# Mixing stage of a hybrid diffusion block: attention denominators moved within a pair, GLA tiles before the last centring, last transposes inside the output product, weight splits and loads moved

## The chip, the cores and the metric

The kernel runs on one NeuronCore of a Trainium2 chip. The metric is the device time of one execution in microseconds (us). An execution of its own was also recorded by the hardware profiler; every duration below is from that execution.

## The reference

Two layers, each a feed-forward sublayer, a token-mixing sublayer and a second feed-forward sublayer, over 256 latent tokens and 256 context tokens of width 1024. What matters here is the mixing:

```python
def token_mixing(u, uc, ...):
    pl, pc = split_cols(u @ w_in + b_in), split_cols(uc @ w_in + b_in)
    y_a = windowed_attention(q, k, v, kc, vc, sink)        # 8 heads of 64, softmax with a sink
    y_b = silu(pl[6]) * head_layernorm(o_b, gla_g)          # gated linear attention, 4 heads
    y_c = sigmoid(pl[13]) * head_layernorm(o_c, mlstm_g)    # mLSTM, 4 heads, both directions
    y = concatenate([y_a, y_b, y_c]) @ w_out
```

The softmax divides by the sum of the exponentials and the exponential of the sink. In the first layer the latent and the context tokens are both mixed (T = 512); in the second only the latent tokens are wanted (T = 256). All is float32; the large products are made of three products of float32r halves (a high part and a remainder).

## The kernel before

The kernel is one block with a program for each engine; the programs meet at counting semaphores and nowhere else, so the order within each engine is written out by hand. Weights come in units of at most 128x2048: SyncE loads a unit into one of two `raw` buffers (unit n into n % 2), ScalarE copies it to `w_hi` (`split_hi`, L300), VectorE subtracts to make `w_lo` (`split_lo`, L308) and increments `lo_ready`, which lets SyncE load unit n + 2 and TensorE begin unit n. `split_lo` waits for the `hi_ready` of its own `split_hi`.

A layer's mixing sublayer has three parts. **project**: 21 tiles of `u @ w_in`, with the GLA work between them (`gla_after`), until ScalarE has evicted tile 20 (L765). With tile 20, the last, ScalarE and VectorE also split the first unit of w_out. **mixing**: N = 16 iterations in the first layer, N = 8 in the second, over query blocks of 128 tokens (qb) and pairs of attention heads (j = 0 to 3). Four iterations of one qb are what is called a pair below. **project_out**: eight output tiles, each 24 matmuls into bank 4 or 5, in the order of `OUT_ORDER` (inputs 4, 5, 0 to 3, 6, 7; 4 and 5 are GLA, 0 to 3 attention, 6 and 7 mLSTM).

One iteration i of mixing, by engine:
- TensorE: at i % 4 == 1, from i = 5, `denominators` (L1887, sixteen recorded matmuls that turn the inverse sums of the previous qb) at the start; then `scores(i)` (L1849); `turn(i-1)` (L1861, transposes of the exponentials into banks 2 and 3); `values(i-2)` (L1876); mLSTM `keys_queries` (L1901) and `numerators` (L1919). In the first layer a head takes four iterations, with `keys_queries(h, 0..2)` and `numerators(2h), (2h+1)`; in the second a head takes two, and `numerators` stand ahead of `turn`.
- VectorE: `outputs(qb-1)` at j == 2 (L1170, values times inverse sums, to `y_att`), `heads_done` (L1201 to L1211) when a `numerators` is there, the row maxima of the scores (L1251, L1254), the mLSTM `weights` (L1222, L1226), `turned(i-1)` (L1149), `inverses` (L1162, L1164), `centred` (L1176 to L1184, a layer norm's first half).
- ScalarE: at j == 1 `denominators(qb-1)` first (L859, bank 2 to `den_inv`), the two exponentials (L897), `turned(i-1)` (L847), and `decays` (L873 to L880, the mLSTM decay weights of one head and direction).
- GpSimd makes `xg` from `g_all` (L629), which SyncE spreads from a row in memory (`spread`, L475). Each spread of direction d waits until the decays before it are done (`w_ready`).

`denominators` and `turn` share bank 2. That is why `turn(4)`, `turn(8)`, ... (the first of a qb) wait for `den_ready`, the eviction at L859:

```python
if g == 0:
    wait(pe, m["den_ready"], (i - 4) // Q_TILES + 1 if i % Q_TILES == 0 else 0)
```

The tail, after the last iteration. TensorE: `turn_out(4)`, `turn_out(5)` (L1926, transposes of the GLA outputs), `denominators` of the last qb, the last `values`, then a wait for `y_tok_ready`, `turn_out(6)`, a wait for `yt_full`, `turn_out(7)`, and only then project_out, which waits for `att_ready`. ScalarE: the sigmoid of the gate (L908), the last L859, the square root of the mLSTM variances (L911), and the high parts `u_hi` (L920) in `OUT_ORDER`. VectorE: `heads_done(7)`, `centred(3)`, `gated_out(4)`, `gated_out(5)` (L1305), `outputs` of the last qb, reciprocal and normalization (L1320, L1323, `y_tok`), `low` (L1312, the remainders `u_lo`) of 4, 5, 0, 1, 2, 3, `gated_out(6)`, `gated_out(7)`, `low(6)`, `low(7)`.

SyncE: w_out unit 0, then two spreads, unit 1, unit 2, then the six other spreads, unit 3.

Of the kernel before, what the change touches and what calls it, by code (L numbers as in the profile page):

```python
# [13 lines left out]
P = 128  # L14
# [103 lines left out]
def hybrid_block_kernel(nc, x, c, ctx_in, c_ctx, ada_w, ada_b, norm_g, ffn1_wg, ffn1_wu, ffn1_wd, ffn2_wg, ffn2_wu,  # L118
# [3 lines left out]
    with ExitStack() as stack:  # L122
# [257 lines left out]
        TURN_BANKS = {4: 5, 5: 6, 6: 7, 7: 5}  # L380
# [16 lines left out]
        def _(sp):  # L397
# [46 lines left out]
            for layer in range(DEPTH):  # L444
# [34 lines left out]
                for u in range(KT // 2):  # L479
# [5 lines left out]
                    if u == KT // 2 - 1:  # L485
                        for hd in range(2, 2 * C_HEADS):
                            spread(hd)
# [169 lines left out]
        def _(act):  # L657
# [92 lines left out]
            def project(layer, m, T):  # L750

                n0 = first_unit["in", layer]
                for t in range(N_PROJ):
                    u = t // 2
                    if t % 2 == 0 and t > 0:
                        split_hi(act, n0 + u + 1)
# [78 lines left out]
            def mixing(layer, m, T):  # L835
# [50 lines left out]
                for i in range(N):  # L886
                    qb, j = i // Q_TILES, i % Q_TILES
                    W = TOK if qb < 2 else CTX
                    if j == 1 and qb > 0:
                        denominators(qb - 1)  # L890
# [8 lines left out]
                    if i >= 1:  # L899
                        turned(i - 1)  # L900
                    h, step = (i + lead) // per_head, (i + lead) % per_head
# [8 lines left out]
                act.wait_ge(m["ml_ln"], 5 * C_HEADS)  # L910
                nc.scalar.activation(ml_s[:, 2, :, 0:NQ], ml_s[:, 1, :, 0:NQ], ACT.Sqrt, bias=eps_col[:], scale=1.0 / 64)\  # L911
                    .then_inc(m["ml_sqrt"], 1)
                for f in OUT_ORDER:
                    if f < Q_TILES:
                        act.wait_ge(m["att_ready"], NQ)
                        src = y_att[:, f, 0:T]
                    else:
                        act.wait_ge(m["yt_full"], f - 3)
                        src = tmp_b[f % 2][:, 0:T]
                    nc.scalar.activation(u_hi[:, f, 0:T], src, ACT.Copy).then_inc(m["yt_hi"], 1)  # L920
# [59 lines left out]
        def _(dve):  # L980
# [152 lines left out]
            def mixing(layer, m, T):  # L1133
# [103 lines left out]
                for i in range(N):  # L1237
# [24 lines left out]
                    if per_head == 4:  # L1262
# [13 lines left out]
                        if step == 2 and h > 0:  # L1276
                            centred(h - 1)
                    if per_head == 2 and step == 1 and h < C_HEADS:
# [19 lines left out]
                centred(C_HEADS - 1)  # L1298
# [19 lines left out]
                outputs(NQ - 1)  # L1318
                dve.wait_ge(m["ml_sqrt"], 1)
# [7 lines left out]
                for f in (4, 5, 0, 1, 2, 3):  # L1327
                    low(f)
# [24 lines left out]
            def project(layer, m, T):  # L1353

                n0 = first_unit["in", layer]
                for t in range(N_PROJ):
                    if t % 2 == 0 and t > 0:
                        split_lo(dve, n0 + t // 2 + 1)
# [192 lines left out]
        def _(pe):  # L1551
# [261 lines left out]

            def project_out(layer, m, z, T):
                n0 = first_unit["out", layer]
                pe.wait_ge(m["att_ready"], T // P)
                for u in range(KT // 2):
                    s = begin(n0 + u)
                    for t in range(2 * u, 2 * u + 2):
                        wait(pe, post["y_ready"], KT * z + t - 1)  # L1820
                        for e, k in enumerate(OUT_ORDER):
                            if t == 0:
# [7 lines left out]
            def mixing(layer, m, T):  # L1830
# [21 lines left out]
                def turn(i):  # L1852

                    n = 4 if i // Q_TILES < 2 else 2
                    for g in range(A_GROUPS):
                        pe.wait_ge(m["exp_done"], 2 * i + g + 1)
                        wait(pe, m["pt_dve"] if g else m["pt_act"], i)
                        if g == 0:
                            wait(pe, m["den_ready"], (i - 4) // Q_TILES + 1 if i % Q_TILES == 0 else 0)
# [20 lines left out]
                def denominators(qb):  # L1880

                    pe.wait_ge(m["den_step"], 2 * qb + 2)
                    pe.wait_ge(m["pt_act"], Q_TILES * (qb + 1))
# [39 lines left out]
                def turn_out(f):  # L1923

                    for tt in range(NQ):
                        last = nc.tensor.transpose(bank[TURN_BANKS[f]][:, tt * P:(tt + 1) * P],  # L1926
                                                   y_tok[:, tt, (f - Q_TILES) * P:(f - Q_TILES + 1) * P], ident[:])
                    last.then_inc(m["yt_turned"], 1)

# [12 lines left out]
                for i in range(N + 2):  # L1942
                    h, step = (i + lead) // per_head, (i + lead) % per_head
                    if i % Q_TILES == 1 and i >= Q_TILES:
                        denominators(i // Q_TILES - 1)
                    if i < N:
                        scores(i)
                    if i == 0:
                        turn_values()
# [13 lines left out]
                    if i == N:  # L1963
                        pe.wait_ge(m["p_ready"], pair_done(T, C_HEADS - 1, n_groups - 1, 1))
                        turn_out(4)
                        turn_out(5)
                    if per_head == 4 and step > 0 and h < C_HEADS:
# [6 lines left out]
                pe.wait_ge(m["y_tok_ready"], 2 * (T // LAT))  # L1974
                turn_out(6)
                pe.wait_ge(m["yt_full"], 1)
                turn_out(7)
# [104 lines left out]
```

## Time and profile before

| | us |
|---|---|
| median of 3 runs (2002.73 to 2006.70) | 2004.55 |
| profiled execution, its own time | 2008.94 |
| profiled execution, span from first to last instruction | 2007.1 |
| TensorE busy | 1873.5 (93%) |
| VectorE busy | 1109.3 (55%) |
| ScalarE busy | 760.1 (38%) |
| GpSimd busy | 243.6 (12%) |

The mixing iterations of the first layer run from 604.5 to 707.7 us of the span, those of the second from 1698.1 to 1751.9 us; the eight tiles of project_out follow each. Feed-forward work fills nearly all of the rest. The time of a row is where an instruction begins. A duration is that of the whole merged group (x4 is four instructions), and the value in brackets is how long the engine had been idle, with what released it. The granted clock is 1.00 at 2.4 GHz and 0.50 at 1.2 GHz.

### The profile page before, as it was taken

Reading aid. Unit: us, or ns where it says so; the run is one execution under the profiler, and the core shown is the slowest. Engines: PE = TensorE matmul, PEld = TensorE weight load, DVE = VectorE, ACT = ScalarE, POOL = GpSimd, SP = SyncE. Lnnn points to the kernel's source line nnn. Section 1 sums busy time; section 2 is a strip of 40 time slices with the busy share of each in tenths; the row PEclk is TensorE's granted clock in tenths of the full one; section 3 lists DMA queues with packets and bytes.
Section 4 is the critical chain, followed back from the end, with each engine's and each line's share of the span. In section 5 each row is a group of like instructions: output and inputs, shape, how many; then the busy total and the mean of one; then the engine's idle time right before and its main releaser. Section 6 shows DMA issues by size and latency. Waiting matters only on the chain. (4 is left out here: it accounts for less than half of the span.)

```text
span 2007.1 us, 25666 instructions
## 1 busy us (share of the span) xinstructions
PE 1873.5 (93%) x10461; PEld 1521.9 (76%) x10461; DVE 1109.3 (55%) x1630; ACT 760.1 (38%) x1132; POOL 243.6 (12%) x327
## 2 busy tenths in 40 slices
PE   5999999979998886999999979999999799879998
PEld 3788877857786664888778858887888488769997
DVE  1777722245756646777522267775222676855544
ACT  4423222236436445222313253222232645654443
POOL 4011110012531000111110001110000152000000
PEclk7999999989999797999999979999999799979999
DMA  9566654342321022666553416665234243036654
GB/s 298 147 180 196 178 160 141 96 113 43 85 64 43 11 63 63 202 178 191 168 173 87 115 49 202 178 194 153 79 94 113 65 106 84 13 105 165 178 166 122
DMA packets 366469, 254.05 MB, mean 127 GB/s; under 512 B 30610, under 2 KB 343276, under 8 KB 366352
## 3 DMA queue, kind: packets, MB, share of 16 engines
q1 hardware_dynamic: 345648, 182.97, 33.1%
q0 software_dynamic: 20704, 69.44, 10.8%
q8 instruction: 83, 1.36, 0.3%
q14 instruction: 34, 0.28, 0.0%
HBM read 251.30 MB, written 1.07 MB: 126 GB/s over the span
## 5 line engine op out<-in xcount | busy, mean ns | idle before, releaser
L324 PE MATMUL bank<-u_hi,w_hi 128*128 128x512 f32 (+2 forms) x1872 | 690.8, 369 | 29.7 <-DVE u_lo L1000 20.6
L325 PE MATMUL bank<-u_lo,w_hi 128*128 128x512 f32 (+2 forms) x1872 | 682.8, 365 | 0.0
L326 PE MATMUL bank<-u_hi,w_lo 128*128 128x512 f32 (+2 forms) x1872 | 682.5, 365 | 0.0
L308 DVE TENSOR_TENSOR w_lo<-raw,w_hi 128x2048 fp32r<-128x2048 f32 (+2 forms) x182 | 373.0, 2049 | 262.3 <-ACT w_hi L300 262.1
L324 PEld LDWEIGHTS bank<-u_hi,w_hi 128*128 128x128 f32 (+1 forms) x1872 | 357.8, 191 | 110.8 <-issue 51.6
L326 PEld LDWEIGHTS bank<-u_hi,w_lo 128*128 128x128 f32 (+1 forms) x1872 | 357.5, 191 | 56.8 <-issue 0.9
L325 PEld LDWEIGHTS bank<-u_lo,w_hi 128*128 128x128 f32 (+1 forms) x1872 | 358.1, 191 | 53.8 <-issue 0.5
L300 ACT ACTIVATE w_hi<-raw 128x2048 fp32r<-128x2048 f32 (+2 forms) x182 | 311.8, 1713 | 144.0 <-PE bank L326 126.6
L324 PE MATMUL bank<-ht_hi,w_hi 128*128 128x512 f32 (+1 forms) x704 | 256.8, 365 | 1.4 <-DVE w_lo L308 1.4
L326 PE MATMUL bank<-ht_hi,w_lo 128*128 128x512 f32 (+1 forms) x704 | 255.3, 363 | 0.0
L325 PE MATMUL bank<-ht_lo,w_hi 128*128 128x512 f32 (+1 forms) x704 | 255.2, 363 | 0.0
L715 ACT ACTIVATE tmp_a<-bank 128x512 f32<-128x512 f32 (+1 forms) x88 | 47.9, 544 | 537.1 <-PE bank L326 537.1
L1034 DVE SCALAR_TENSOR_TENSOR ada_sum<-ada_slot,silu_c,ada_sum 128x512 f32<-128x512 f32 x336 | 230.7, 746 | 0.0
L512 POOL DMA_DIRECT2D ada_slot<-in_ada_w_dram x128 | 92.1, 720 | 936.3 <-DVE ada_sum L1034 655.1
L1053 DVE TENSOR_TENSOR tmp_b<-bank,tmp_a 128x512 f32<-128x512 f32 (+1 forms) x88 | 55.0, 625 | 210.9 <-ACT tmp_a L715 210.9
L324 PEld LDWEIGHTS bank<-ht_hi,w_hi 128*128 128x128 f32 x704 | 132.8, 189 | 27.6 <-issue 6.7
L326 PEld LDWEIGHTS bank<-ht_hi,w_lo 128*128 128x128 f32 x704 | 132.8, 189 | 20.7
L325 PEld LDWEIGHTS bank<-ht_lo,w_hi 128*128 128x128 f32 x704 | 132.9, 189 | 20.4
L724 ACT ACTIVATE tmp_a<-bank 128x512 f32<-128x512 f32 (+1 forms) x48 | 25.3, 527 | 206.6 <-PE bank L326 206.6
L1075 DVE TENSOR_TENSOR tmp_b<-tmp_b,tmp_a 128x512 f32<-128x512 f32 (+1 forms) x36 | 21.7, 604 | 124.0 <-ACT tmp_a L724 124.0
L1056 DVE TENSOR_TENSOR ht_lo<-tmp_b,ht_hi 128x512 fp32r<-128x512 f32 (+1 forms) x88 | 55.1, 626 | 56.7 <-ACT ht_hi L717 56.7
L717 ACT ACTIVATE ht_hi<-tmp_b 128x512 fp32r<-128x512 f32 (+1 forms) x88 | 50.9, 578 | 61.1 <-DVE tmp_b L1053 61.1
(244 smaller groups left out, 1486.4 us busy)
## 6 DMA issues: line engine op xcount, KB each, us to landing
ada_slot<-in_ada_w_dram POOLq DMA_DIRECT2D x128, 512.0 KB, 4.7
raw<-in_ffn_wg_dram SPq DMA_DIRECT2D x88, 512.0 KB, 4.8
raw<-in_ffn_wu_dram SPq DMA_DIRECT2D x88, 512.0 KB, 6.2
raw<-in_ffn_wd_dram SPq DMA_DIRECT2D x64, 384.0 KB, 3.4
raw<-in_ffn_wd_dram SPq DMA_DIRECT2D x64, 320.0 KB, 4.0
raw<-in_w_in_dram SPq DMA_DIRECT2D x32, 512.0 KB, 4.3
ada_first<-in_ada_w_dram SPq DMA_DIRECT2D x4, 2048.0 KB, 14.8
raw<-in_w_in_dram SPq DMA_DIRECT2D x16, 256.0 KB, 4.3
```

Of the source, the lines that this page charges most:

```text
L300: nc.scalar.activation(w_hi[s][:, 0:size], raw[s][:, 0:size], ACT.Copy).then_inc(hi_ready[s], 1)
L308: nc.vector.tensor_tensor(w_lo[s][:, 0:size], raw[s][:, 0:size], w_hi[s][:, 0:size].bitcast(F32), ALU.subtract).then_inc(lo_ready[s], 1)
L324: nc.tensor.matmul(acc, wh, xh, start=first, stop=False)
L325: nc.tensor.matmul(acc, wh, xl, start=False, stop=False)
L326: return nc.tensor.matmul(acc, wl, xh, start=False, stop=last)
L512: pool.dma_start(ada_slot[slot][:], src[:, 2 * r:2 * r + 2, b * BLOCK:(b + 1) * BLOCK]).then_inc(ada_loaded[slot], 16)
L715: nc.scalar.activation(tmp_a[j][:, 0:T], bank[2 * j][:, 0:T], ACT.Silu).then_inc(gated["silu_ready"], 1)
L717: nc.scalar.activation(ht_hi[:, f, 0:T], tmp_b[j][:, 0:T], ACT.Copy).then_inc(gated["hthi_ready"], 1)
L724: nc.scalar.activation(tmp_a[b][:, 0:T], bank[4 + b][:, 0:T], ACT.Square).then_inc(post["ysq_ready"], 1)
L1034: ins = nc.vector.scalar_tensor_tensor(acc[:], ada_slot[slot][:, kk, :], c_k, acc[:], ALU.mult, ALU.add)
L1053: nc.vector.tensor_tensor(tmp_b[j][:, 0:T], bank[2 * j + 1][:, 0:T], tmp_a[j][:, 0:T], ALU.mult).then_inc(gated["prod_ready"], 1)
L1056: nc.vector.tensor_tensor(ht_lo[:, f, 0:T], tmp_b[j][:, 0:T], ht_hi[:, f, 0:T].bitcast(F32), ALU.subtract).then_inc(gated["ht_ready"], 1)
```

## The change

1. **Denominators at the end of a pair's first iteration.** TensorE issues them at the end of iteration 5, 9, 13 (and N + 1) and no longer at the start; ScalarE evicts them after `turned(i-1)` and ahead of `decays` (before, ahead of the exponentials by position, but behind the `decays` of the iteration before). The wait for `den_ready` moves from the `turn` of iterations 4, 8, 12 to that of 5, 9, 13, and `outputs` stay at j == 2.
2. **`keys_queries(0, 2)`** moves from the end of iteration 1 to behind `scores(2)`, in the first layer only.
3. **First w_out unit.** Its `split_hi` and `split_lo` leave tile 20 of project for iteration 2 of mixing, in both layers. On ScalarE it stands behind `turned(1)`; on VectorE behind `turned(1)` in the first layer and ahead of `weights` and `turned(1)` in the second.
4. **SyncE** issues the six other spreads ahead of w_out unit 2 (before: behind it).
5. **Tail.** VectorE: `gated_out(4)`, `(5)`, `outputs`, `low` of 4, 5, 0, 1, then `centred(3)`, `low` of 2, 3, then reciprocal and `y_tok`. ScalarE's square root moves behind the `u_hi` of 4, 5, 0 to 3. TensorE's `turn_out(6)` and `(7)` move into the first output tile, between inputs 3 and 6; bank 0 instead of 5 takes the second, and its wait for `yt_full` goes.
6. A second wait for `proj_ready` ahead of `turn_values`; the one ahead of the loop stays.

```diff
-        TURN_BANKS = {4: 5, 5: 6, 6: 7, 7: 5}
+        TURN_BANKS = {4: 5, 5: 6, 6: 7, 7: 0}
...
-                    if u == KT // 2 - 1:
+                    if u == 2:
                         for hd in range(2, 2 * C_HEADS):
                             spread(hd)
...
-                    if t % 2 == 0 and t > 0:
+                    if t % 2 == 0 and 0 < t < N_PROJ - 1:
                         split_hi(act, n0 + u + 1)
...
-                    if j == 1 and qb > 0:
-                        denominators(qb - 1)
                     if j == 0 and qb > 0:
                         sink_terms(qb - 1)
...
                     if i >= 1:
                         turned(i - 1)
+                    if i == 2:
+                        split_hi(act, first_unit["out", layer])
+                    if j == 1 and qb > 0:
+                        denominators(qb - 1)
...
-                act.wait_ge(m["ml_ln"], 5 * C_HEADS)
-                nc.scalar.activation(ml_s[:, 2, :, 0:NQ], ...)
                 for f in OUT_ORDER:
+                    if f == 6:
+                        act.wait_ge(m["ml_ln"], 5 * C_HEADS)
+                        nc.scalar.activation(ml_s[:, 2, :, 0:NQ], ...)
...
                         if step == 2 and h > 0:
                             centred(h - 1)
+                    if i == 2:
+                        split_lo(dve, first_unit["out", layer])
                     if per_head == 2 and step == 1 and h < C_HEADS:
                         weights(h, 0, 0)
...
                 heads_done(2 * C_HEADS - 1)
-                centred(C_HEADS - 1)
...
                 outputs(NQ - 1)
+                for f in (4, 5, 0, 1):
+                    low(f)
+                centred(C_HEADS - 1)
+                for f in (2, 3):
+                    low(f)
                 dve.wait_ge(m["ml_sqrt"], 1)
...
-                for f in (4, 5, 0, 1, 2, 3):
-                    low(f)
...
-                    if t % 2 == 0 and t > 0:
+                    if t % 2 == 0 and 0 < t < N_PROJ - 1:
                         split_lo(dve, n0 + t // 2 + 1)
...
                         for e, k in enumerate(OUT_ORDER):
+                            if t == 0 and k == 6:
+                                pe.wait_ge(m["y_tok_ready"], 2 * (T // LAT))
+                                turn_out(6, T)
+                                turn_out(7, T)
                             if t == 0:
                                 pe.wait_ge(m["yt_ready"], e + 1)
...
-                        if g == 0:
-                            wait(pe, m["den_ready"], (i - 4) // Q_TILES + 1 if i % Q_TILES == 0 else 0)
+                        if g == 0 and i % Q_TILES == 1:
+                            wait(pe, m["den_ready"], i // Q_TILES)
...
-                    pe.wait_ge(m["pt_act"], Q_TILES * (qb + 1))
+                    pe.wait_ge(m["pt_act"], min(Q_TILES * (qb + 1) + 1, N))
...
-                    if i % Q_TILES == 1 and i >= Q_TILES:
-                        denominators(i // Q_TILES - 1)
                     if i < N:
                         scores(i)
+                    if per_head == 4 and i == 2:
+                        keys_queries(0, 2)
                     if i == 0:
+                        pe.wait_ge(m["proj_ready"], N_PROJ)
                         turn_values()
...
-                    if per_head == 4 and step > 0 and h < C_HEADS:
+                    if per_head == 4 and step > 0 and h < C_HEADS and i != 1:
                         keys_queries(h, step - 1)
...
-                pe.wait_ge(m["y_tok_ready"], 2 * (T // LAT))
-                turn_out(6)
-                pe.wait_ge(m["yt_full"], 1)
-                turn_out(7)
+                    if i % Q_TILES == 1 and i >= Q_TILES:
+                        denominators(i // Q_TILES - 1)
```

## Rows read from the trace of the kernel before

**Rows 1.** The page, part 1: busy time (share of the span) xinstructions.

```profile
PE 1873.5 (93%) x10461; PEld 1521.9 (76%) x10461; DVE 1109.3 (55%) x1630; ACT 760.1 (38%) x1132; POOL 243.6 (12%) x327
```

**Rows 2.** Stretches: length, busy PE, PEld, DVE, ACT, POOL, clock, DMA share, GB/s.

```profile
604.50:707.70 103.20, 89.83 (x648) 67.77 (x649) 68.53 (x209) 55.72 (x163) 7.61 (x6) 0.87 0.10 27
612.90:619.80 6.90, 6.90 (x32) 4.72 (x32) 4.17 (x12) 2.65 (x8) 2.53 (x2) 0.53 0.18 40
681.20:701.70 20.50, 20.50 (x98) 16.56 (x98) 8.73 (x31) 5.41 (x14) 0.00 (x0) 0.51 0.01 1
707.70:720.50 12.80, 12.78 (x51) 10.06 (x49) 7.70 (x10) 3.51 (x4) 0.00 (x0) 0.87 0.20 49
1698.10:1751.90 53.80, 48.39 (x417) 38.10 (x417) 44.14 (x150) 35.94 (x94) 4.38 (x6) 1.00 0.14 35
1751.90:1759.40 7.50, 7.47 (x51) 7.27 (x48) 5.42 (x10) 2.78 (x4) 0.00 (x0) 0.77 0.00 1
```

**Rows 3.** Timeline, TensorE, first stage, opening: start, duration, operation, [idle before <-releaser].

```profile
612.79 1.64 PE L1901 MATMUL bank<-qk_conv 64*128 64x256 f32 x3 [2.25 <-DVE w_c L1226]
```

**Rows 4.** Timeline, ScalarE then VectorE, first stage, opening.

```profile
602.05 1.91 ACT L300 ACTIVATE w_hi<-raw 128x2048 fp32r<-128x2048 f32 x1
...
603.99 2.29 DVE L308 TENSOR_TENSOR w_lo<-raw,w_hi 128x2048 fp32r<-128x2048 f32 x1 [3.35 <-ACT w_hi L300]
```

**Rows 5.** Waits of the first stage: total us, times, longest.

```profile
DVE probs_t L1149 <- PE bank L1861: 7.5, 4, 5.9
...
PE bank L1861 <- ACT den_inv L859: 3.5, 3, 1.3
```

**Rows 6.** Timeline, TensorE, ScalarE, VectorE, first stage, around denominators.

```profile
631.93 1.13 PE L1901 MATMUL bank<-qk_conv 64*128 64x256 f32 x4
...
634.15 1.09 PE L1887 MATMUL bank<-ident,row_sum 128*64 128x128 f32 x16 [1.08 <-ACT probs_t L847]
...
639.55 0.48 PE L1901 MATMUL bank<-qk_conv 64*128 64x256 f32 x1 [0.29 <-DVE w_c L1226]
...
636.45 0.58 ACT L859 ACTIVATE den_inv<-bank 128x512 f32<-128x512 f32 x1
...
636.43 0.69 DVE L1251 CUSTOM_DVE_ANT_0 probs<-bank,att_mask 128x512 f32<-128x512 f32 x1 [0.71 <-PE bank L1849]
...
640.61 0.68 DVE L1170 TENSOR_TENSOR y_att<-bank,den_inv 128x512 f32<-128x512 f32 x1
...
678.08 0.76 DVE L1254 TENSOR_REDUCE row_max<-bank 128x1 f32<-128x256 f32 x2 [0.25 <-PE bank L1849]
```

**Rows 7.** Timeline, TensorE then VectorE, first stage, tail.

```profile
706.87 1.09 PE L1926 MATMUL bank<-ident,y_tok 128*128 128x128 f32 x8 [3.68 <-DVE y_tok L1323]
...
707.72 0.48 PE L324 MATMUL bank<-u_hi,w_hi 128*128 128x512 f32 x1
...
714.88 0.39 PE L324 MATMUL bank<-u_hi,w_hi 128*128 128x512 f32 x1
...
711.78 1.35 DVE L1312 TENSOR_TENSOR u_lo<-tmp_b,u_hi 128x512 fp32r<-128x512 f32 x2
```

**Rows 8.** Timeline, ScalarE then VectorE, second stage, opening.

```profile
1711.15 0.57 ACT L847 ACTIVATE probs_t<-bank 128x512 f32<-128x512 f32 x1
...
1709.60 0.62 DVE L1226 SCALAR_TENSOR_TENSOR w_c<-bank,w_c 128x256 f32<-128x256 f32 x2
...
1714.71 0.69 DVE L1251 CUSTOM_DVE_ANT_0 probs<-bank,att_mask 128x512 f32<-128x512 f32 x1
...
1719.94 0.69 DVE L1251 CUSTOM_DVE_ANT_0 probs<-bank,att_mask 128x512 f32<-128x512 f32 x1 [1.00 <-DVE hid_tmp L1211]
```

**Rows 9.** Timeline, TensorE then VectorE, second stage, tail.

```profile
1751.47 0.66 PE L1926 MATMUL bank<-ident,y_tok 128*128 128x128 f32 x4 [2.62 <-DVE y_tok L1323]
...
1756.34 0.28 PE L324 MATMUL bank<-u_hi,w_hi 128*128 128x256 f32 x1
...
1754.31 0.82 DVE L1312 TENSOR_TENSOR u_lo<-tmp_b,u_hi 128x256 fp32r<-128x256 f32 x2
```

More of the change, by code:

```diff
@@ L909, in mixing @@
                 denominators(NQ - 1)
-                act.wait_ge(m["ml_ln"], 5 * C_HEADS)
-                nc.scalar.activation(ml_s[:, 2, :, 0:NQ], ml_s[:, 1, :, 0:NQ], ACT.Sqrt, bias=eps_col[:], scale=1.0 / 64)\
-                    .then_inc(m["ml_sqrt"], 1)
                 for f in OUT_ORDER:
+                    if f == 6:
+                        act.wait_ge(m["ml_ln"], 5 * C_HEADS)
+                        nc.scalar.activation(ml_s[:, 2, :, 0:NQ], ml_s[:, 1, :, 0:NQ], ACT.Sqrt, bias=eps_col[:], scale=1.0 / 64)\
+                            .then_inc(m["ml_sqrt"], 1)
                     if f < Q_TILES:
@@ L1812, in gla_after, with turn_out @@
                         last.then_inc(m["gate_turned"], 1)
+            def turn_out(f, T):
+                m = mixer
+                for tt in range(T // P):
+                    last = nc.tensor.transpose(bank[TURN_BANKS[f]][:, tt * P:(tt + 1) * P],
+                                               y_tok[:, tt, (f - Q_TILES) * P:(f - Q_TILES + 1) * P], ident[:])
+                last.then_inc(m["yt_turned"], 1)
             def project_out(layer, m, z, T):
@@ L1921, in numerators @@
                     last.then_inc(m["num_done"], 1)
[L1923 to L1928, printed above, removed]
                 def turn_values():
@@ L1964, in mixing @@
                         pe.wait_ge(m["p_ready"], pair_done(T, C_HEADS - 1, n_groups - 1, 1))
-                        turn_out(4)
-                        turn_out(5)
-                    if per_head == 4 and step > 0 and h < C_HEADS:
+                        turn_out(4, T)
+                        turn_out(5, T)
+                    if per_head == 4 and step > 0 and h < C_HEADS and i != 1:
                         keys_queries(h, step - 1)
```

## The prediction

> **What bounds the kernel.** I read the page first: TensorE is busy 93% of the span [rows 1], so only what TensorE waits for can be had. Then the stretches of both mixing stages: the first is 103.2 us with TensorE busy 89.8 of them at a granted clock of 0.87, the second 53.8 us with 48.4 busy at 1.00 [rows 2]. The change touches only these stages and the first output tile behind each. The idle time, 13.4 and 5.4 us, is the direct stake, and the clock a second one: the first stage holds two stretches at 1.2 GHz, 6.9 us and 20.5 us long, in which TensorE is shown as busy throughout [rows 2]. Then the waits and the timelines, engine by engine. At the ends of the pairs and in both tails TensorE waits for VectorE or ScalarE, which wait for TensorE in turn, so a step has to be followed through the three queues.
>
> **Opening of the first stage.** keys_queries(0, 2) makes TensorE wait 2.25 us for VectorE's weights with scores(2) ready behind it, and then the clock is at 0.53 for 6.9 us [rows 2, 3]. With scores(2) ahead, the gap shrinks to some 0.4 us in pieces: 1.9 us gained. If the clock then stays up, the 6.9 us at 0.53 become 3.8: 3.1 more. Against that stands the split of the first w_out unit, now in iteration 2: 1.91 us on ScalarE and then 2.29 us on VectorE, which has to wait for it [rows 4]. Queued behind it on VectorE is heads_done(0). TensorE meanwhile has scores(3), turn(2), values(1) and keys_queries(1, 0), four groups of about 1.1 us [rows 6], and comes to numerators(1), which need heads_done(0), at the same moment; on ScalarE the exponentials of iteration 4 come to stand behind decays(2) and lose 1.0. Leaving tile 20 gains 0.1: the eviction of tile 20 waits for its matmuls anyway, and TensorE's start hangs on that; what goes from VectorE there (2.29 us) has TensorE's own turn_values and keys_queries as its cover. Sum: -1.9 - 3.1 + 1.0 = **-4.0 us** (bounds: -5.0, and 0 if the clock falls all the same and the stall costs more).
>
> **Denominators, first stage, three times.** Removed: TensorE's wait for the 0.58 us eviction, which stands behind decays on ScalarE (3.5 us in three), and the 1.08 us and its like ahead of L1887 [rows 5, 6]. But TensorE only reaches keys_queries(h, 2) sooner, and that waits for VectorE's weights(h, 0, 1) as it does now (idle 0.29 [rows 6]). VectorE gains where it waited for the late scores and turns: 0.71, 0.25, and three waits of 1.6 together (7.5 less the longest, 5.9, which belongs to the tail): 2.6 in all [rows 5, 6]. It loses at outputs: these now follow keys_queries (1.05), denominators (1.05) and the eviction (0.58 and 0.1 of handing over), 2.8 us behind weights(h, 0, 1), where it has 1.1 us of its own (639.55 to 640.61 [rows 6]). That is 1.7 us of new waiting each time, and the row maxima, the weights of the third group and numerators are queued behind it. 3 x 1.65 - 2.55 = **+2.4 us** (bounds: +5, and -3.5 if only the removed wait counted).
>
> **Tail of the first stage.** VectorE's queue sets it: today it runs without a gap to the last remainder, 711.78 + 1.35 = 713.1, and the second output tile starts at 714.88 [rows 7]. Its instructions are the same; two waits are new. centred(3), some 2.1 us, was the cover for denominators and their eviction; now outputs stand there, and values(15) comes ahead of denominators: 1.4 us of waiting. Then y_tok to turn_out(6) to gated_out(6), now without the remainders as a cover: 0.6. The output product does start earlier (about 705.2 for 707.72 [rows 7]), but its inputs 6 and 7 come last and later: last remainder 715.1, second tile at 715.9: **+1.0 us** (bounds: -2.5, the earlier start kept whole; +2.5).
>
> **Opening of the second stage.** Here split_lo stands ahead of weights(1, 0, 0), which starts at 1709.60. ScalarE comes to split_hi at 1711.15 + 0.5 [rows 8]; 1.91 and 2.29 us [rows 4] end at 1715.8. So VectorE is 6.2 us late. A wait for the transposes absorbs some 0.5, the idle 1.00 ahead of 1719.94 [rows 8] nearly all of another microsecond; the rest passes from max(3) (1714.71 [rows 8]) to everything behind it, since each engine waits for the one before: **+4.8 us** (bounds: 0, cover after all; +6.2). What it leaves in project (the split in tile 20) ran beside that tile's matmuls: 0. TensorE, ready for numerators(2) at 1713.3, stands until 1717.0, 3.7 us. The gaps of 2.25, 3.68 and 2.62 us [rows 3, 7, 9] were each followed by some time at 1.2 GHz: the stretches at 0.53, 0.87 and 0.77 [rows 2]. So I price a clock fall here at what it costs if it is as short as the first: TensorE's three groups before it needs VectorE again take 3.6 us more, of which 1.7 lies in a wait: **+1.9 us** (bounds: 0, and +9 if it is like the stretch of 20.5 us).
>
> The Trainium skill's page "TensorE: Matmul & The Clock Gate" (Why this matters for your kernels) asks for no long idle gap between bursts of matmuls, and its part on a second failure mode says that short idles between groups can make the clock swing too. The trace agrees with the second: 2.25 us was enough.
>
> **Second stage, the rest.** Denominators once: outputs are 1.1 us later, but the scores behind them come late too; **0** (bounds +-1.1). Tail: the same two waits, 1.3 and 0.5 us; the last remainder goes from 1754.31 + 0.82 to 1756.9, the second tile from 1756.34 [rows 9] to 1757.3: **+1.0 us** (bounds: -1.5, +2).
>
> **SyncE, GpSimd and the doubled wait: 0.** The six spreads no longer stand behind w_out unit 2 and its load; xg comes earlier. Unit 2 now loads behind the last spread, half a stage later, and has the second half of mixing and the products of two w_out units as cover; if that were not enough, TensorE would wait ahead of the fifth output tile. The second wait for proj_ready is behind one that it repeats.
>
> **Sum.** -4.0 + 2.4 + 1.0 + 4.8 + 1.9 + 0 + 1.0 = **+7.1 us**. The profiled execution took 2008.94 us (span 2007.1), 0.2% above the median; I add the sum to the median: 2004.55 + 7.1 = **2011.6 us**, +0.35%. A measurement of this kernel can tell about 0.2% (4.0 us) from no change.
>
> **Rivals.**
> - *The clock stays up* (faster). The place is the first stage from 681 us on: 20.5 us at 0.51, TensorE busy all the time [rows 2]. At 1.00 this is 10.2 us less, and with no fall in the second stage 1.9 less again: 2011.6 - 12.1 = 1999.5. For it: the gaps ahead of L1887 and of turn at the third pair end go. Against: in their place comes one of some 2.4 us ahead of keys_queries(h, 2), and the 2.25 us gap was followed by a fall. It decides if no gap of more than 2 us is followed by one. 0.15.
> - *The clock falls more often.* There are three gaps of 2.2 to 2.6 us now in the first stage and 3.7 in the second, each a candidate by the same rows; one further stretch like that of 20.5 us costs 10: 2021. By the skill's advice on idle gaps this is the danger of the change. 0.15.
> - *The split in the second stage is covered* (the wait costs nothing): 2011.6 - 4.8 - 1.9 = 2004.9. For: VectorE is busy 44 of 53.8 us, not all [rows 2]. Against: ScalarE cannot start it before 1711.6, and VectorE's queue waits in order. 0.12.
> - *The tails gain what they are meant to*, the product's earlier start: -2.5 and -1.2 for +1.0 and +1.0: 2005.9. Against: VectorE's queue has no gap to lose today. 0.08.
> - *It does not do what it says*: only the doubled wait, which does nothing; no time in it.
>
> **Chances and range.** The forecast has 0.50; its own range is 2006 to 2016, and 0.08 of the 0.50 lies within 0.2% of 2004.55. Slower by over 0.2%: 0.42 of it and the 0.15 of the second rival, 0.57. Faster: 0.11 of the first rival's 0.15 (its 1999.5 is 0.25% below) and 0.03 of the third's, 0.14. Within 0.2%: 0.08, 0.04, 0.09 of the third and the 0.08 of the fourth, 0.29. The range, 2001 to 2020, takes in both covers and most of one long fall, and leaves out the better half of the first rival and the worse half of the second.
>
> **What would show it.** In the first stage: no gap of 2 us ahead of L1901 at its start, numerators(0) 5 us sooner; VectorE waiting for den_inv ahead of L1170 by 1.5 us three times. In the second: VectorE idle for 4 us ahead of L308, and TensorE idle for 3 to 4 us ahead of L1919. In the tails: TensorE starts L324 sooner by 2.5 and 1 us, then waits for u_lo, and the second tile starts 1 us later against turned of the last iteration. I am wrong if VectorE does not wait in the second stage, or if the stretches at 1.2 GHz change their sum by more than 7 us.

## The result and the profile after

The changed kernel took 2018.71 us (median of 4 runs, 2016.79 to 2024.21), the kernel before 2004.03 us beside it (2002.73 to 2006.70). The ratio is 1.0076, 95% interval 1.0054 to 1.0098: slower by 14.7 us, inside the range of the prediction, 7.1 us above its forecast. The recorded execution took 2024.21 us.

The page of the changed kernel, span and part 1:

```profile
span 2022.4 us, 25670 instructions
PE 1879.8 (93%) x10461; PEld 1522.8 (75%) x10461; DVE 1110.3 (55%) x1630; ACT 761.3 (38%) x1132; POOL 243.6 (12%) x327
```

The number of instructions is that of [rows 1] on every engine, and DVE and ACT are busy 1.0 and 1.2 us more. PE is busy 6.3 us more with the same 10461 matmuls, so more of them ran at the lower clock; the rest of the 15.3 us that the span grew is waiting. Stretches of the changed kernel: first stage up to the first output product, two short pieces of it, that product; then the second stage likewise. The short pieces are windows set around stretches at 1.2 GHz and begin 0.4 us after them (length, busy PE, PEld, DVE, ACT, POOL, clock, DMA share, GB/s):

```profile
607.50:702.10 94.60, 81.77 (x640) 59.70 (x640) 66.03 (x199) 55.09 (x159) 7.61 (x6) 0.95 0.11 29
640.50:643.90 3.40, 3.40 (x16) 1.56 (x13) 1.56 (x4) 0.60 (x1) 0.65 (x1) 0.56 0.00 0
684.90:688.30 3.40, 3.40 (x23) 2.32 (x23) 0.55 (x2) 0.60 (x1) 0.00 (x0) 0.56 0.00 0
702.10:721.90 19.80, 14.41 (x56) 10.84 (x57) 11.86 (x21) 7.83 (x13) 0.00 (x0) 0.91 0.20 54
1699.20:1761.50 62.30, 52.61 (x412) 41.60 (x412) 44.20 (x143) 35.65 (x92) 4.36 (x6) 0.92 0.11 31
1719.10:1725.90 6.80, 6.22 (x38) 5.88 (x38) 6.17 (x21) 2.58 (x8) 0.72 (x1) 0.53 0.02 4
1761.50:1775.00 13.50, 10.39 (x52) 9.61 (x52) 8.05 (x19) 5.96 (x12) 0.00 (x0) 0.62 0.10 25
```

The kernel before, each stage from its first scores to the start of the third output tile, where TensorE waits for the eviction of the first (Y_mix):

```profile
604.50:721.90 117.40, 102.61 (x696) 77.83 (x696) 76.65 (x219) 60.61 (x170) 7.61 (x6) 0.87 0.12 32
1698.10:1760.30 62.20, 55.86 (x464) 45.39 (x465) 49.86 (x160) 39.61 (x100) 4.38 (x6) 0.97 0.12 31
```

**The first stage became shorter, the second much longer.** Up to the third output tile the first takes 114.3 us for 117.4, clock 0.95 in its loop for 0.87; the second takes 75.8 us (1699.28 to 1775.06) for 62.2. That is -3.1 and +13.6 of the 15.3 us. The rest lies outside of the change: +3.0 ahead of the first stage, +1.3 between the stages and +0.5 behind. There the two recorded executions differ in their stretches at 1.2 GHz: 15 us more of them in all in the changed kernel (mean granted clock 0.949 for 0.953), none of it in the two stages.

The second stage's loss starts in its third iteration. Timeline of the changed kernel, ScalarE, then VectorE, then TensorE:

```profile
1712.80 1.90 ACT L300 ACTIVATE w_hi<-raw 128x2048 fp32r<-128x2048 f32 x1
...
1714.73 2.29 DVE L308 TENSOR_TENSOR w_lo<-raw,w_hi 128x2048 fp32r<-128x2048 f32 x1 [3.87 <-ACT w_hi L300]
1716.94 0.62 DVE L1229 SCALAR_TENSOR_TENSOR w_c<-bank,w_c 128x256 f32<-128x256 f32 x2
...
1719.24 0.29 DVE L1210 TENSOR_TENSOR hid_tmp<-bank,c_den 128x128 f32<-128x128 f32 x1
...
1721.78 0.69 DVE L1254 CUSTOM_DVE_ANT_0 probs<-bank,att_mask 128x512 f32<-128x512 f32 x1
...
1719.68 3.22 PE L1938 MATMUL bank<-vm_tok,w_c 128*128 128x65 f32 x14 [5.08 <-DVE hid_tmp L1210]
1722.70 1.91 PE L1880 MATMUL bank<-ident,probs 128*128 128x128 f32 x8
```

VectorE idles 3.87 us for ScalarE's half of the split, then works 2.29 us on its own, and everything of the iteration stands behind both: the row maxima of iteration 3 (L1254) start 22.5 us into the stage, before 16.6. TensorE idles 5.08 us, and what it waits for at the end is `hid_tmp` of heads_done(1) at 1719.24, six entries behind the weights at 1716.94 in VectorE's queue. The clock falls while it still waits, at 1718.7, and stays at 1.2 GHz for 6.8 us.

At the ends of the pairs in the first stage, TensorE and VectorE of the changed kernel ([rows 6] show the same place before: L1901 is now L1920, L1887 is L1906, L1170 is L1173):

```profile
638.47 1.13 PE L1920 MATMUL bank<-qk_conv 64*128 64x256 f32 x4 [2.04 <-DVE w_c L1229]
639.53 1.46 PE L1906 MATMUL bank<-ident,row_sum 128*64 128x128 f32 x16
640.92 2.08 PE L1868 MATMUL bank<-proj 64*128 64x512 f32 x4
...
641.65 0.69 DVE L1173 TENSOR_TENSOR y_att<-bank,den_inv 128x512 f32<-128x512 f32 x1 [2.05 <-ACT den_inv L859]
...
662.83 1.13 PE L1920 MATMUL bank<-qk_conv 64*128 64x256 f32 x4 [2.68 <-DVE w_c L1229]
...
683.77 1.41 PE L1920 MATMUL bank<-qk_conv 64*128 64x256 f32 x4 [1.97 <-DVE w_c L1229]
```

The waits ahead of L1887 and of turn are gone, and TensorE waits 2.0 to 2.7 us ahead of keys_queries(h, 2) instead of 0.29. Each of the three is followed by a stretch of 3.4 us at 1.2 GHz (from 640.1, 664.0 and 684.5; two stand in the stretches above). The long one of 20.5 us [rows 2] is not there. Waits (total us, times, longest) of the same kernel in that stage:

```profile
DVE y_att L1173 <- ACT den_inv L859: 7.6, 4, 2.8
```

### The profile page after: what moved, and what is told of

Same layout as the page of the kernel before. It is cut to its first block and busy times, and to the rows that moved or that the text cites. A ratio compares the mean times of both kernels' runs of the same rounds, so it can differ in the third digit from the quotient of the medians.

```text
span 2022.4 us, 25670 instructions
## 1 busy us (share of the span) xinstructions
PE 1879.8 (93%) x10461; PEld 1522.8 (75%) x10461; DVE 1110.3 (55%) x1630; ACT 761.3 (38%) x1132; POOL 243.6 (12%) x327
## 5 line engine op out<-in xcount | busy, mean ns | idle before, releaser
L308 DVE TENSOR_TENSOR w_lo<-raw,w_hi 128x2048 fp32r<-128x2048 f32 (+2 forms) x182 | 373.0, 2050 | 262.4 <-ACT w_hi L300 262.1
L325 PEld LDWEIGHTS bank<-ht_lo,w_hi 128*128 128x128 f32 x704 | 132.9, 189 | 20.5
L326 PEld LDWEIGHTS bank<-ht_hi,w_lo 128*128 128x128 f32 x704 | 132.8, 189 | 20.5
```

The lines of the kernel that those rows point to most:

```text
L308: nc.vector.tensor_tensor(w_lo[s][:, 0:size], raw[s][:, 0:size], w_hi[s][:, 0:size].bitcast(F32), ALU.subtract).then_inc(lo_ready[s], 1)
L325: nc.tensor.matmul(acc, wh, xl, start=False, stop=False)
L326: return nc.tensor.matmul(acc, wl, xh, start=False, stop=last)
```

## The experiments

All are compared with runs of the kernel before on the same chip. Times and ratios are from all runs; stage times are from the one recorded execution of each kernel, in two parts: the loop, from the stage's first scores to VectorE's last copy of transposed exponentials, and the tail, from there to the third output tile. Kernels measured on different chips are compared by their ratios.

**The split alone, and everything but the split.** e1 is the changed kernel with the split back in tile 20:

```diff
-                    if t % 2 == 0 and 0 < t < N_PROJ - 1:
+                    if t % 2 == 0 and t > 0:
...
-                    if i == 2:
-                        split_hi(act, first_unit["out", layer])
...
-                    if i == 2:
-                        split_lo(dve, first_unit["out", layer])
```

> The changed kernel with the first w_out unit split in tile 20 of project again, in both layers; all else as changed. Theory S (VectorE's wait for ScalarE's split ahead of weights in the second mixing stage is the largest part of the loss: max(4) came 7.9 us later against the first scores): the time falls by 7 to 10 us from the changed kernel's 2018.7, to 2009 to 2012, and TensorE's gap of 5.1 us ahead of numerators(2) is gone. Rival C (the loss is in the clock and in the tails, wherever the split stands): falls by less than 3 us, to 2016 or more.

e2 is the opposite: these edits, and the order of the spreads, on the kernel before.

> The kernel before with the split in iteration 2 of mixing in both layers, and the spreads ahead of w_out unit 2; nothing else. Theory S: slower than before by 6 to 10 us (2010 to 2014), nearly all of it in the second stage, where VectorE waits some 4 us for the split. In the first stage TensorE still waits ahead of keys_queries(0, 2), so the stall costs up to 1 to 2 us there. Rival C: within 3 us of 2004.

Measured: e1 2009.87 us, ratio 1.0025 (1.0010 to 1.0040), for 1.0076 of the changed kernel: without the split 8.8 us of the 14.7 are gone by the medians, some 10 us by the ratios. e2 2016.86 us, 1.0060 (1.0040 to 1.0080): alone it costs 12 us. In e1 the second stage takes 68.2 us, 7.6 less than in the changed kernel. In e2 the second stage takes 56.5 + 14.9 us for 47.3 + 14.9 of before: +9.2, all of it in the loop. Its timeline, VectorE then TensorE, repeats what the changed kernel showed (L1209 is heads_done here):

```profile
1708.97 2.29 DVE L308 TENSOR_TENSOR w_lo<-raw,w_hi 128x2048 fp32r<-128x2048 f32 x1 [3.87 <-ACT w_hi L300]
...
1713.92 3.22 PE L1923 MATMUL bank<-vm_tok,w_c 128*128 128x65 f32 x14 [5.09 <-DVE hid_tmp L1209]
```

**The tail alone, and everything but the tail.** e3 is the changed kernel with part 5 of the change taken back, e4 the kernel before with part 5 alone. The core of e4:

```diff
-                centred(C_HEADS - 1)
...
+                for f in (4, 5, 0, 1):
+                    low(f)
+                centred(C_HEADS - 1)
+                for f in (2, 3):
+                    low(f)
...
+                            if t == 0 and k == 6:
+                                pe.wait_ge(m["y_tok_ready"], 2 * (T // LAT))
+                                turn_out(6, T)
+                                turn_out(7, T)
```

> The changed kernel with the tail of before (centring, y_tok and the last transposes ahead of the output product). Theory T (the new tail costs 1 us in each stage by VectorE's two new waits, and some of the clock on top: from the last turned the second output tile came 1.5 and 2.3 us later): faster than the changed kernel by 2 to 5 us, 2014 to 2017. Rival (the tail gains its earlier start of the output product, and the losses behind it are the clock's own): slower than the changed kernel by 0 to 3 us.

> The kernel before with the new tail alone. Theory T: slower than before by 1.5 to 4 us (2005.5 to 2008): VectorE waits for den_inv ahead of L1170 about 0.8 to 1.4 us and for turn_out(6) 0.8 to 1 us, in both stages. Here denominators still stand ahead of the last values, so the first of these waits is shorter by up to 1 us than in the changed kernel. Rival: faster by 2 to 4 us, as the output product starts 2.5 and 1.2 us earlier.

Measured: e3 2016.84 us, 1.0066 (1.0047 to 1.0084), some 2 us better than the changed kernel, within what the runs can tell. The expectation had 2 to 5 us. e4 2014.24 us, 1.0038 (1.0015 to 1.0062), its twelve times in two groups: five of 1999.0 to 2006.8 us at granted clocks of 0.960 to 0.962, and seven of 2011.4 to 2022.0 us at 0.950 to 0.956. The recorded execution is of the first (2003.9 us). In it the second tail takes 17.0 us for 14.9, +2.1; the first takes 23.0 us, what it took before. Two more records of the same kernel, e9 and e10 below, have 18.0 and 24.6 us, +3.1 and +1.7. In both, a stretch at 1.2 GHz falls on the second output tile of the first tail; in e4 it lies earlier, where TensorE waits. TensorE's gaps in that second tail:

```profile
1742.11 0.35 PE L324 MATMUL bank<-u_hi,w_hi 128*128 128x256 f32 x1 [1.29 <-DVE u_lo L1312]
...
1744.85 0.38 PE L324 MATMUL bank<-u_hi,w_hi 128*128 128x256 f32 x1 [1.09 <-DVE u_lo L1312]
...
1748.08 0.58 PE L324 MATMUL bank<-u_hi,w_hi 128*128 128x256 f32 x1 [1.32 <-DVE u_lo L1312]
```

One wait of 2.62 us for y_tok [rows 9] became three for remainders, 3.7 us together: TensorE starts the product earlier and still waits for VectorE's remainders.

**The denominators alone.** e5 is the kernel before with part 1 of the change:

```diff
-                    if i % Q_TILES == 1 and i >= Q_TILES:
-                        denominators(i // Q_TILES - 1)
                     if i < N:
                         scores(i)
...
+                    if i % Q_TILES == 1 and i >= Q_TILES:
+                        denominators(i // Q_TILES - 1)
```

> The kernel before with the denominators moved, alone. Theory D (in its new place the chain keys_queries, denominators, eviction, outputs leaves TensorE a gap of 2 to 2.7 us ahead of keys_queries(h, 2) and VectorE a wait of 1.7 us ahead of outputs): slower than before by 3 to 7 us, of which 2 to 3 us are the waits and the rest the clock after the gaps; in the second stage, up to the last turned, 0 to 1 us. Rival (the removed wait for the eviction, 3.5 us in three, is gained): faster by 2 to 4 us.

Measured: 2011.01 us, 1.0030 (1.0018 to 1.0041). Timeline of e5, TensorE in the first stage:

```profile
616.28 1.46 PE L1901 MATMUL bank<-qk_conv 64*128 64x256 f32 x3 [2.25 <-DVE w_c L1226]
642.00 1.13 PE L1901 MATMUL bank<-qk_conv 64*128 64x256 f32 x4 [2.18 <-DVE w_c L1226]
666.48 1.13 PE L1901 MATMUL bank<-qk_conv 64*128 64x256 f32 x4 [2.79 <-DVE w_c L1226]
```

The first row is the old gap of the opening [rows 3]; the others are new. And VectorE waits 7.1 us in three ahead of L1170:

```profile
DVE y_att L1170 <- ACT den_inv L859: 7.1, 3, 2.7
```

The second stage takes 48.7 + 16.3 us: +1.3 in the loop and +1.4 in the tail. The cost by the ratio is 6.0 us, by the medians 7.6.

**keys_queries(0, 2) alone.**

```diff
+                    if per_head == 4 and i == 2:
+                        keys_queries(0, 2)
...
-                    if per_head == 4 and step > 0 and h < C_HEADS:
+                    if per_head == 4 and step > 0 and h < C_HEADS and i != 1:
```

> The kernel before with keys_queries(0, 2) behind scores(2), alone. Theory K: TensorE's gap of 2.25 us ahead of L1901 falls to some 0.5 us, faster than before by 1 to 4 us (1.9 us of waiting, and 0 to 3 of the clock). Rival: no change, since VectorE and not TensorE sets the pace there.

Measured: 2000.66 us, 0.9986 (0.9973 to 0.9998): the one part that gains, some 2.8 us. TensorE's 2.25 us gap is now in two pieces:

```profile
613.08 1.13 PE L1901 MATMUL bank<-qk_conv 64*128 64x256 f32 x4 [0.75 <-DVE w_c L1226]
617.32 2.44 PE L1919 MATMUL bank<-vm_tok,w_c 128*128 128x65 f32 x20 [0.90 <-DVE w_c L1226]
```

The first stage's loop takes 83.8 us in it. In e2 and e4, which have the old opening, it takes 85.1, so the move is worth 1.3 us of that loop.

**Is it the clock or VectorE's queue?** e7 is the changed kernel with seven products that nobody uses in TensorE's 5.1 us gap of the second stage, so that TensorE does not stand still there:

```diff
+                        if i == 3:
+                            pe.wait_ge(m["pt_act"], 2)
+                            for r in range(7):
+                                nc.tensor.matmul(bank[T_BANK][:, 0:TOK], ident[:], proj[:, T_K, :], start=True, stop=True)
```

> The changed kernel, in whose second stage TensorE runs seven idle products of 128x512 (identity by keys into bank 2, some 3.7 us) in the gap of 5.1 us ahead of numerators(2), so that only the clock can change. If the clock's fall is part of what the split costs (9.2 us up to the last turned, where the wait alone is worth some 5.5 to 6): faster than the changed kernel by 2 to 4 us, and TensorE's first numerators after the gap take 1.8 us instead of 3.2. If the fall comes all the same or costs nothing, as VectorE sets the pace: within 1 us.

e8 is the changed kernel with VectorE's half of the split at the end of iteration 2 in place of ahead of the weights:

```diff
-                    if i == 2:
-                        split_lo(dve, first_unit["out", layer])
                     if per_head == 2 and step == 1 and h < C_HEADS:
                         weights(h, 0, 0)
...
+                    if i == 2:
+                        split_lo(dve, first_unit["out", layer])
```

> The changed kernel with VectorE's half of the split at the end of iteration 2 (behind weights, turned, heads_done and centred of the second stage); ScalarE's half stays. Theory S (it is the wait of VectorE for ScalarE, with weights and turned queued behind it, not the 2.29 us of the subtraction): faster than the changed kernel by 5 to 8 us; the wait of 3.9 us ahead of L308 is gone and TensorE's gap ahead of numerators(2) too. Rival (any place in the second stage costs the same, as VectorE is the bound there): faster by less than 3 us.

TensorE of e7 in the gap, and VectorE then TensorE of e8:

```profile
1709.47 6.28 PE L1974 MATMUL bank<-proj,ident 128*128 128x512 f32 x14
1715.58 1.67 PE L1938 MATMUL bank<-vm_tok,w_c 128*128 128x65 f32 x14
1717.09 1.04 PE L1880 MATMUL bank<-ident,probs 128*128 128x128 f32 x8
```

```profile
1714.42 2.29 DVE L308 TENSOR_TENSOR w_lo<-raw,w_hi 128x2048 fp32r<-128x2048 f32 x1
...
1719.24 1.77 PE L1920 MATMUL bank<-qk_conv 64*128 64x256 f32 x7 [2.50 <-DVE w_c L1229]
```

In e7 the clock stays up: the numerators behind the gap take 1.67 us and not 3.22. The first row maxima of iteration 4 are done 29.2 us into the stage, where the changed kernel has 31.0 and the kernel before 23.2. But the stage ends only 1.2 us sooner, though it holds 10 us less at 1.2 GHz. The time is 2018.30 us, 1.0060 (1.0045 to 1.0076): by the ratios up to 3 us better than the changed kernel, which the runs can't tell from nothing. The test is not a clean one: the products took 6.28 us and not the expected 3.7, so the numerators start 1.0 us later against the stage's start than in the changed kernel. Without that the clock could be worth up to 1.0 us more (an estimate from these two starts). In e8 VectorE has no wait at the split, TensorE's gap is 2.50 us, the loop takes 52.3 us for 56.9, and the time is 2015.90 us, 1.0055 (1.0037 to 1.0073), between its two expectations. **VectorE's queue carries the loss; the clock adds 1 to 2 us here, 3 at most.** Even in a better place the split costs: the row maxima of iteration 3 come 2.2 us later in e8 than before, which is the 2.29 us of the instruction itself. The rest of what e8's second stage loses, 8.9 us in all, is not taken apart; it holds the moved denominators and the new tail too.

**The two groups of e4.** The same kernel, recorded twice more.

> The kernel before with the tail edits alone, once more, for its profile. Its twelve timed runs lay in two groups, 1999 to 2006 us and 2014 to 2022 us, and the one recorded execution was of the first group (2003.9 us, granted clock 0.960; second stage 47.5 us to its last transposed exponentials, 2.1 us more than before from there to the second of project_out's units). Theory C (the clock alone makes the second group): a recorded execution of the second group has the same stages within 1 us wherever the granted clock is the same, and the 12 us more are stretches at 1.2 GHz, some 24 us of them more in all. Theory T (the tail edit itself has two outcomes): the 12 us lie behind the last iteration of one of the two stages, at an unchanged clock. If this execution is of the first group, nothing is decided.

> The same kernel and the same two theories as the run before it: by theory C an execution near 2017 us differs from one near 2004 us by some 24 us more at 1.2 GHz, wherever they lie; by theory T the 12 us lie behind the last iteration of one of the stages at the same clock. Two executions of the first group would leave it open.

2006.52 and 2011.60 us. Neither is near 2017, so the groups stay unexplained. What they show is what the clock does with equal work. TensorE in the second stage of e4's record, and then the same place in e9:

```profile
1734.68 1.75 PE L1934 MATMUL bank<-vm_tok,w_c 128*128 128x65 f32 x14 [1.94 <-DVE hid_tmp L1212]
```

```profile
1735.36 2.91 PE L1934 MATMUL bank<-vm_tok,w_c 128*128 128x65 f32 x13 [1.93 <-DVE hid_tmp L1212]
```

The stretch of e9 that begins there:

```profile
1735.80:1742.60 6.80, 6.80 (x41) 6.09 (x40) 1.90 (x8) 2.51 (x3) 0.00 (x0) 0.52 0.01 2
```

One and the same gap was followed by no fall in e4 and by 6.8 us at 1.2 GHz in e9 and e10; their loop takes 49.5 us for 47.5. And e9 and e10 are equal within 0.1 us in every part of both stages; the 5.1 us between them lie ahead of the first stage, where e10 spends 10.2 us more at 1.2 GHz. That is as the theory of the clock has it, for 5 us and not for 12. It is not so everywhere: e9 has 3.4 us at 1.2 GHz (from 694.4) at the start of the first tail that e10 has not, and both tails take 24.6 us, since TensorE has waits there.

**A better place for the eviction, and the split in one layer.** e11 has keys_queries(0, 2) as e6 and, on ScalarE alone, `denominators(qb - 1)` right behind `turned(i - 1)` at j == 0 in the first layer:

```diff
-                    if j == 1 and qb > 0:
+                    if j == 1 and qb > 0 and per_head == 2:
                         denominators(qb - 1)
...
+                    if j == 0 and qb > 0 and per_head == 4:
+                        denominators(qb - 1)
```

> The kernel before with two edits: keys_queries(0, 2) behind scores(2), as in the run that had this alone (2000.7 us, ratio 0.9986), and in the first stage ScalarE evicts the denominators right behind the turned of the last iteration of a pair, ahead of its decays, while TensorE issues them where it did before. Theory D (the 1.1 us gaps ahead of the first turn of a query block, three of them, are a real loss): 2 to 3 us less than with the first edit alone, 1998 us. Theory V (VectorE and ScalarE set the pace there, and the eviction in its new place makes ScalarE wait for TensorE with its decays behind it): the same as the first edit alone or up to 3 us more, 2000 to 2004 us, with new gaps ahead of keys_queries.

e12 has the split in iteration 2 in the first layer only, and the spreads' order in both:

```diff
-                    if t % 2 == 0 and t > 0:
+                    if t % 2 == 0 and 0 < t < N_PROJ - (T == TOK):
...
+                    if i == 2 and T == TOK:
+                        split_lo(dve, first_unit["out", layer])
```

> The kernel before with the split of the first w_out unit moved to iteration 2 of mixing in the first layer alone; in the second layer it stays with tile 20. The six spreads go ahead of w_out unit 2 in both. With the move in both layers it was 2016.9 us (ratio 1.0060). Theory S (the whole cost of the move lies in the second stage): the second stage is back at 47.3 us to its last transposed exponentials, and the time is that of the kernel before, 2002 to 2007 us. Rival (the order of the spreads and loads, or the first stage, costs too): 2008 us or more, with the second stage or project_out waiting for a load.

e11: 2012.06 us, 1.0027 (1.0008 to 1.0046), worse than both theories had it. TensorE's gaps of its first stage:

```profile
638.08 0.48 PE L1903 MATMUL bank<-qk_conv 64*128 64x256 f32 x1 [0.86 <-DVE w_c L1228]
...
660.48 0.91 PE L1903 MATMUL bank<-qk_conv 64*128 64x256 f32 x3 [1.52 <-DVE w_c L1228]
664.67 2.45 PE L1921 MATMUL bank<-vm_tok,w_c 128*128 128x65 f32 x20 [1.47 <-DVE w_c L1228]
...
681.39 0.79 PE L1903 MATMUL bank<-qk_conv 64*128 64x256 f32 x1 [1.96 <-DVE w_c L1228]
```

The 1.3 us ahead of turn are gone and stand ahead of keys_queries(h, 2) again: in this kernel as in e5 and the changed one, the wait taken from TensorE there comes back ahead of VectorE's weights. This record also has the 20.5 us stretch, from 681.2, at the end of the last of these gaps, and its loop takes 94.7 us. e12: 2003.08 us, 0.9990 (0.9974 to 1.0006), no difference, and the loop of its second stage takes 47.7 us, near the 47.3 of before. In the first layer the split and the order of spreads and loads cost nothing that the runs can tell, though VectorE waits there too (2.20 us at its `split_lo`):

```profile
623.63 2.29 DVE L308 TENSOR_TENSOR w_lo<-raw,w_hi 128x2048 fp32r<-128x2048 f32 x1 [2.20 <-ACT w_hi L300]
```

The fastest kernel is e6, faster than the one before by 0.14% (at least 0.02%) and faster than the changed one by 18 us.

## Why the prediction was right, and where it was not

The sign and the range were right, with 14.7 us for the forecast's 7.1. By its own steps:

**Opening of the second stage, +4.8 and +1.9.** The mechanism was the right one and the largest term: ScalarE's half late, VectorE waiting 3.87 us ahead of L308 ("idle for 4 us") and then working. The size was off: 9.2 us in e2 for 6.7. Two steps failed. "A wait for the transposes absorbs some 0.5, the idle 1.00 nearly all of another microsecond": nearly nothing is absorbed of the 6.2 us. In e2 the row maxima of iteration 3 come 5.9 us later than before, and in e7, with the clock held up, those of iteration 4 still 6.0 us later. And "TensorE, ready for numerators(2), stands until 1717.0, 3.7 us" named the weights as the last thing awaited, where it is heads_done(1), six instructions further down VectorE's queue: 5.08 us. The clock term, +1.9, has the right size: 6.8 us at 1.2 GHz followed, and e7 puts its worth at 1.2 (end of the stage) to 1.9 us (row maxima of iteration 4), or up to 1.0 more for the products' late end.

**Second stage, the rest, 0 and +1.0.** Together they were too low. "Outputs are 1.1 us later, but the scores behind them come late too" holds for the loop within its bound (+1.3 in e5). But denominators at the end of iteration N + 1 also delay the tail by 1.4 us, which had no term of its own. The tail term was counted to the second output tile; there e4 is 1.2 us later than before, near the forecast's 1.0, and the changed kernel 2.3. To the third tile e4 loses 2.1 us. Split, denominators and tail measured alone make 9.2 + 2.7 + 2.2 = 14.1 us in this stage; together they made 13.6. So in these records the parts add up. That rests on which record of the tail edits is taken: in e9 and e10 they cost the stage 5.3 us and not 2.2, with 6.8 us more at 1.2 GHz.

**Denominators in the first stage, +2.4.** The step was right: TensorE would "only reach keys_queries(h, 2) sooner", and VectorE would wait for den_inv. The waits are larger: 2.4 us each in e5 (7.1 in three) where I had 1.7, and 2.0 to 2.7 us ahead of keys_queries. The cost by the ratio is 6.0 us for e5, less 2.7 for the second stage: some 3.3. By the recorded loops it depends on what it is held against: 92.4 us in e5 against 94.5 before, or against 85.1 in e4 and e9, which have the loop of before unchanged.

**That is the trap of the base.** The recorded execution of before had the stretch of 20.5 us at 0.51 [rows 2], and the same loop without it takes 85.1 us, 9.3 less. I noted that this execution was 0.2% above the median and used the stretch as a rival's stake, but it comes and goes between executions: e4, e9 and e10, with the same loop, don't have it, nor have e2 and e6; e11 and e12 do. The kernel before itself was recorded only once. So the first stage of the changed kernel looks 3.1 us better than before in the two profiles, while its loop takes 4.3 us more than that of e4, and by the runs only the move of keys_queries gains anything there.

**Opening of the first stage, -4.0.** Right in sign. (6.9 us at 0.53 are 3.7 us at full clock, so the -3.1 should have been -3.2; nothing hangs on it.) The split's +1.0 is 0 (85.12 us in e2 with it, 85.10 in e4 without; e12 0.9990). Of the gain, -1.9 and -3.1, the runs show -2.8 together with bounds of -0.4 and -5.4 (e6). **Tail of the first stage, +1.0**: to the second tile 0.0 in e4 and +1.5 us in the changed kernel; to the third 0.0 in e4 and +1.7 in e9 and e10. The term is about as large as what the clock does to it. **SyncE and the doubled wait, 0**: right for the spreads (e12); the wait was not tried by itself.

**What does not add up.** By the ratios the four parts measured alone make 12.0 (split) + 6.0 (denominators) + 7.6 (tail) - 2.8 (keys_queries) = 22.8 us, together 15.2. Most of the difference is in the tail edits: 7.6 us when they stand alone, 2.0 when they are taken out of the changed kernel (e3). No run shows why, and e4's two groups belong to the same open question. So it is in part luck that the measured time lies in the forecast's range: the second stage was forecast at +7.7 us and took +13.6, and the first, forecast at -0.6, shows -3.1 against the record of before and +6.2 against that of e4.

**The rivals.** "The clock stays up" did not come: in the recorded execution the long stretch was not there, and short ones were. Up to the third output tiles the two stages have seven, 34 us together, where the kernel before had four, also 34 us: so the net loss between the two profiles in these stages is not a longer time at 1.2 GHz. By this the prediction's own sign of being wrong (a change of more than 7 us) is not met in the stages; outside of them it is, with 15 us more, and 4.8 us of the span. "It falls more often" named the mechanism that did come, with gaps of 2.0 to 2.7 and 5.1 us all followed by a fall, and its 2021 is nearer to the result than the forecast; but its further long stretch did not come, and e7, which held the clock up at the longest gap, did not change the time beyond what the runs can tell. The Trainium skill's page "TensorE: Matmul & The Clock Gate" (Why this matters for your kernels) advises against long idle gaps; here the clock stayed at 1.00 when the 5.1 us gap was filled with products that do nothing, and no time clear of the noise came back. "The split is covered" was excluded for the second layer by e2 beside e12, and held in the first; "the tails gain" was excluded by e4, whose ratio is above 1 by its whole interval.

## What to carry to other kernels

A pair of instructions on two engines, the second waiting for the first, costs the second engine's in-order queue the whole wait plus its own time: put it where that queue idles, and look in each layer separately, since the same move was free in one and cost 9 us in the other, its clock fall included. To price such a stall, follow the queue to the last thing that the third engine needs, not the first. And before a trace is used as a base, compare its stretches at the lower clock with a second record of the same code: here a loop took 94.5 us in one record and 85.1 in three others.

## What the runs showed of the hardware

The same instructions of one kernel with the same gap (1.93 and 1.94 us) were followed by a fall of the granted clock in two executions and by none in a third. Over the 68 runs of the kernel before beside the experiments, the time (1999 to 2014 us) follows the mean granted clock, some 1.4 us for 0.001 of it (a straight line through them). In one place the effect was seen alone: 10.2 us more at 1.2 GHz ahead of the first stage of e10 than of e9, 5.1 us more time. In another, 3.4 us at 1.2 GHz made no difference. Why e4 has two groups 12 us apart stays open. Their mean clocks are 0.961 and 0.954; by the line that would be 10 of the 12 us, but a line through other runs does not say which of the two causes the other.
